# Five places in the order of work, earlier norms of the memory queries, and eight sums of squares in fp32r pairs

## The reference, cut to what matters

```python
def rms_norm(x, g):
    return x * lax.rsqrt(jnp.mean(x * x, axis=-1, keepdims=True) + NORM_EPS) * g

qa = partial_rope(rms_norm(q_a, moba_q_norm[l]), positions)      # mq: head queries
ka = partial_rope(rms_norm(k_a, moba_k_norm[l]), positions)      # mk: head keys
o_a = moba_attention(qa, ka, v_a)                                # moba
o_h = rms_norm(hgrn2_chunkwise(q_h, f_h, i_h, lb), hgrn_o_norm[l])   # ho
qm = rms_norm(q_m, mem_q_norm[l])                                # sq: memory queries
km = rms_norm(k_m, mem_k_norm[l])                                # sk: memory keys
o_m = memory_attention(qm, km, v_m)                              # matt
y = concatenate([o_a, o_h, o_m]) * silu(z)
x = x + y @ w_out[l]
```

## Time and profile before

| | |
|---|---|
| three runs, median (lowest to highest) | 1533.81 us (1533.65 to 1534.88) |
| the profiled execution | 1533.24 us |
| its span, first to last instruction | 1531.3 us |
| granted TensorE clock over the span | 1.00 |
| PE, busy share of the span | 98% |
| DVE | 76% |
| ACT | 50% |
| POOL | 7% |

### The profile page before, as it was taken

One profiled execution on the slowest core, in us unless ns is written; L12 is line 12 of the kernel. 1 busy time (PEld: TensorE's weight loads), 2 busy tenths in 40 slices (PEclk: granted clock), 3 DMA queues, 4 the chain that ended last, 5 costly groups with the idle time before them and its releaser, 6 DMA issues.

```text
span 1531.3 us, 23925 instructions
## 1 busy us (share of the span) xinstructions
PE 1495.4 (98%) x9958; PEld 1343.6 (88%) x9958; DVE 1170.6 (76%) x1392; ACT 763.8 (50%) x937; POOL 100.0 (7%) x70
## 2 busy tenths in 40 slices
PE   8999999999999999999999999999999989999988
PEld 6888899989888888888998888888999869999967
DVE  7878768757887778877677788777779676589774
ACT  5434456535433463334555544345565675555673
POOL 2000010011000010000100100001213001103000
PEclk9999999999999999999999999999999999999999
DMA  8655535214655546555433465555444314544302
GB/s 271 216 193 191 168 139 192 83 56 150 220 189 192 191 165 208 182 189 192 164 140 111 157 222 183 195 180 179 149 169 162 106 36 176 207 141 163 110 29 83
DMA packets 51888, 246.76 MB, mean 161 GB/s; under 512 B 4619, under 2 KB 5771, under 8 KB 27718
## 3 DMA queue, kind: packets, MB, share of 16 engines
q1 hardware_dynamic: 50662, 238.29, 44.7%
q0 software_dynamic: 1120, 6.96, 1.2%
HBM read 244.18 MB, written 1.05 MB: 160 GB/s over the span
## 4 chain that ended last, share of the span: by engine, by line
PE 82%; DVE 8%; ACT 5%; issue 2%; POOL 0%; DVEq 0%; ACTq 0%
PE ps L1166 20%; PE ps L1168 10%; PE ps L1089 10%; PE ps L1091 10%; PE ps L1090 10%; PE ps L1219 9%; PE ps L1220 4%; PE ps L1383 4%; PE ps L1531 1%; ACT w_hi L1638 1%; DVE w_lo L1964 1%; ACT work L1851 1%; PE ps L1520 1%; DVE act_two L2072 1%; PE ps L1499 1%
## 5 line engine op out<-in xcount | busy, mean ns | idle before, releaser
L1638 ACT ACTIVATE w_hi<-raw 128x2048 fp32r<-128x2048 f32 x184 | 351.4, 1914 | 382.7 <-PE ps L1168 267.0
L1964 DVE TENSOR_TENSOR w_lo<-raw,w_hi 128x2048 fp32r<-128x2048 f32 x177 | 405.1, 2291 | 135.2 <-ACT w_hi L1638 132.9
L1166 PE MATMUL ps<-act_two,w_hi 128*128 128x512 f32 x1408 | 444.7, 397 | 2.6 <-DVE xn L1973 1.3
L1168 PEld LDWEIGHTS ps<-act_two,w_lo 128*128 128x128 f32 x1408 | 265.3, 188 | 63.1
L1089 PE MATMUL ps<-act_two,w_hi 128*128 128x256 f32 x1088 | 318.8, 293 | 1.0 <-DVE w_lo L1958 0.9
L1091 PE MATMUL ps<-act_two,w_lo 128*128 128x256 f32 x1088 | 307.7, 283 | 0.0
L1090 PE MATMUL ps<-act_two,w_hi 128*128 128x256 f32 x1088 | 307.7, 283 | 0.0
L1168 PE MATMUL ps<-act_two,w_lo 128*128 128x256 f32 x1408 | 277.4, 278 | 0.0
L1166 PEld LDWEIGHTS ps<-act_two,w_hi 128*128 128x128 f32 x1408 | 215.3, 189 | 5.3 <-DVE xn L1973 1.7
L1089 PEld LDWEIGHTS ps<-act_two,w_hi 128*128 128x128 f32 x1088 | 208.6, 192 | 5.8 <-issue 5.1
L1090 PEld LDWEIGHTS ps<-act_two,w_hi 128*128 128x128 f32 x1088 | 208.7, 192 | 4.2 <-issue 4.1
(11 more groups left out here) (294 smaller groups left out, 2065.0 us busy)
## 6 DMA issues: line engine op xcount, KB each, us to landing
raw<-panels SPq DMA_DIRECT2D x184, 1024.0 KB, 4.8
raw<-panels SPq DMA_DIRECT2D x80, 512.0 KB, 4.9
raw<-panels SPq DMA_DIRECT2D x8, 256.0 KB, 6.5
table<-tab POOLq DMA_DIRECT2D x1, 1472.0 KB, 8.9
table<-tab POOLq DMA_DIRECT2D x1, 1216.0 KB, 5.5
xn<-x_in SPq DMA_DIRECT2D x4, 256.0 KB, 4.3
work<-mem_in POOLq DMA_DIRECT2D x1, 1024.0 KB, 9.1
xn<-mem_in POOLq DMA_DIRECT2D x1, 1024.0 KB, 5.3
```

The costliest lines, as they stand in the source:

```text
L1166: pe.matmul(grid(ps[:, bank + half], 2), w[half][0], act_two[:, slots[c]], start=c == 0, stop=False)
L1168: ins = pe.matmul(ps[:, bank + half, 0:SEQ], w[half][1], act_hi[:, slots[c]], start=False, stop=c == DC - 1)
L1638: nc.scalar.activation(w_hi[:, s], raw[:, s], ACT.Copy).then_inc(panel_hi, 1)
L1964: tt(w_lo[:, s], raw[:, s], w_hi[:, s].bitcast(F32), ALU.subtract).then_inc(panel_lo, 1)
```

## The change

1. Mixer 0: cn_sq of dq 0 is moved from behind the table load to the round of the last convolution, in front of conv_silu 4.
2. Mixer 1: norm_sum and rstd of mix1 are moved ahead of the first half of panel 1.
3. Mixer 1: scores of dilated heads 0 and 1 move one round on, behind the half panel (10, 1); the two cn_sum of fo move in front of attend of dilated heads 0 and 1.
4. Last mixer, layer 1: diagonal and diagonal_in move one round on, behind both halves of panel 7 and gap_f 0.
5. Last mixers: the norms of sq leave paired_heads and become a strand of their own from round n + 4, in front of the strand of mq, mk and ho. Their sums are written to banks 2 and 3 and wait for rope of mq 1 and of mk 1.
6. The sums of mq and mk, eight in all, are made of two fp32r products: ACT makes the Square twice, once rounded to fp32r (into g_two) and once plain, POOL subtracts to get the rest (cn_lo), and PE multiplies both with ones in fp32r (ones_r, made once beside wab_hi).
7. Every cn_sq now waits for the cn_sum two before it in the order.

```diff
+NORM_PARTS = [("pe", "cn_sum", 1), ("act", "cn_sq", 0), ("pool", "cn_lo", 0), ("act", "cn_rstd", 1), ("dve", "cn_use", 1)]
@@ hgrn_rounds
+    late = out.pop() if l else []
+    out += [[]] * l
     ahead = len(out)
...
+    out[ahead] = out[ahead] + late
@@ paired_heads
-    out[0] += pair(0, ("pe", "scores")) + [("act", "evacuate", (f"in2_{l}", 19))] + norm("cn_sq", 0, 1) + norm("cn_sum", 0, 1)
+    out[0] += pair(0, ("pe", "scores")) + [("act", "evacuate", (f"in2_{l}", 19))]
...
-        if p in (0, 1):
-            out[a] += norm("cn_rstd", p)
-        if p in (1, 2):
-            out[a] += norm("cn_use", p - 1)
@@ last_mixer
-              [[]] * n + rounds(NORM_COLS, qk + [(f"ho{l}", 0), (f"ho{l}", 1)]),
+              [[]] * (n + 4) + rounds(NORM_COLS, [(f"sq{l}", 0), (f"sq{l}", 1)]),
+              [[]] * n + rounds(NORM_PARTS, qk + [(f"ho{l}", 0), (f"ho{l}", 1)]),
...
+    chains[2] = [[x for x in r if x[1] != "cn_lo" or x[2][0] in qk] for r in chains[2]]
@@ order, mixer 0
-    conv_end = [[], [], [("dve", "conv", (5,)), ("act", "conv_silu", (4,)), ("act", "conv_silu", (5,)), ("act", "logs", ())]]
-    out += weave(conv_end + delta_rounds()[1:], halves(panel_list("in0", None, 6)), BESIDE_0)
+    conv_end = [[], [], [("dve", "conv", (5,)), ("act", "cn_sq", (("dq", 0),)), ("act", "conv_silu", (4,)), ("act", "conv_silu", (5,)), ("act", "logs", ())]]
+    rest = [[x for x in r if x != ("act", "cn_sq", (("dq", 0),))] for r in delta_rounds()[1:]]
+    out += weave(conv_end + rest, halves(panel_list("in0", None, 6)), BESIDE_0)
@@ order, mixer 1
-    out += first[:1] + [("pe", "half", ("in1", 1, 0)), ("pe", "norm_sum", ("mix1",)), ("act", "rstd", ("mix1",)), ("pe", "half", ("in1", 1, 1))]
+    out += first[:1] + [("pe", "norm_sum", ("mix1",)), ("act", "rstd", ("mix1",)), ("pe", "half", ("in1", 1, 0)), ("pe", "half", ("in1", 1, 1))]
...
-    dilated = [[]] * 4 + [two(0, ("pe", "scores")), two(0, ("dve", "mask_max"), ("act", "exp")),
+    dilated = [[]] * 5 + [two(0, ("pe", "scores")) + two(0, ("dve", "mask_max"), ("act", "exp")),
...
-                          two(0, ("pe", "attend")) + two(1, ("dve", "mask_max"), ("act", "exp")),
+                          pair(("pe", "cn_sum")) + two(0, ("pe", "attend")) + two(1, ("dve", "mask_max"), ("act", "exp")),
...
-    norms = [pair(("act", "cn_sq")), pair(("pe", "cn_sum"), ("act", "cn_rstd")), pair(("dve", "cn_use")), [("dve", "gate_out", (("dil", 0),))]]
+    norms = [pair(("act", "cn_sq")), pair(("act", "cn_rstd")), pair(("dve", "cn_use")), [("dve", "gate_out", (("dil", 0),))]]
@@ GpSimd
+            def cn_lo(unit):
+                i = norm_index[unit] % 2
+                pool.wait_ge(act_done, at("act", "cn_sq", unit))
+                hi, lo = sq_parts[i]
+                nc.gpsimd.tensor_tensor(lo, sq[i], hi.bitcast(F32), ALU.subtract).then_inc(pool_done, 1)
@@ TensorE, cn_sum
                 if unit[0][:2] == "sq":
-                    pe.wait_ge(act_done, at("act", "evacuate", "in2_" + unit[0][2], 18 + unit[1]))
+                    pe.wait_ge(dve_done, at("dve", "rope", (("mq", "mk")[unit[1]] + unit[0][2], 1)))
+                if unit in in_parts:
+                    pe.wait_ge(pool_done, at("pool", "cn_lo", unit))
+                    one, (hi, lo) = ones_r[:, int(unit[0][0] == "m")], sq_parts[norm_index[unit] % 2]
+                    pe.matmul(ps[:, bank], one, hi, start=True, stop=False)
+                    pe.matmul(ps[:, bank], one, lo, start=False, stop=True).then_inc(pe_done, 1)
+                    return
@@ ScalarE, cn_sq
+                if norm_index[unit] >= 2:
+                    act.wait_ge(pe_done, at("pe", "cn_sum", norm_list[norm_index[unit] - 2]))
...
+                if unit in in_parts:
+                    nc.scalar.activation(grid(sq_parts[norm_index[unit] % 2][0], 2), src, ACT.Square)
```

More of the change, by code:

```diff
@@ L412, in paired_heads @@
     pair = lambda p, *steps: [(e, k, ((f"moba{l}", h),)) for e, k in steps for h in (2 * p, 2 * p + 1)]
-    norm = lambda kind, *groups: [("pe" if kind == "cn_sum" else "dve" if kind == "cn_use" else "act", kind, ((f"sq{l}", g),)) for g in groups]
-    out[0] += pair(0, ("pe", "scores")) + [("act", "evacuate", (f"in2_{l}", 19))] + norm("cn_sq", 0, 1) + norm("cn_sum", 0, 1)
+    out[0] += pair(0, ("pe", "scores")) + [("act", "evacuate", (f"in2_{l}", 19))]
     for p in range(4):
@@ L539, in order @@
     heads = rounds(SCORES_FIRST, [("dif", h) for h in range(4)])
+    pair = lambda *steps: [(e, k, (("fo", g),)) for e, k in steps for g in (0, 1)]
     two = lambda p, *steps: [(e, k, (("dil", h),)) for e, k in steps for h in (2 * p, 2 * p + 1)]
-    dilated = [[]] * 4 + [two(0, ("pe", "scores")), two(0, ("dve", "mask_max"), ("act", "exp")),
+    dilated = [[]] * 5 + [two(0, ("pe", "scores")) + two(0, ("dve", "mask_max"), ("act", "exp")),
                           two(1, ("pe", "scores")) + two(0, ("dve", "divide"), ("pe", "turn_p"), ("act", "p_cols")),
-                          two(0, ("pe", "attend")) + two(1, ("dve", "mask_max"), ("act", "exp")),
+                          pair(("pe", "cn_sum")) + two(0, ("pe", "attend")) + two(1, ("dve", "mask_max"), ("act", "exp")),
                           two(1, ("dve", "divide"), ("pe", "turn_p"), ("act", "p_cols")), two(1, ("pe", "attend"))]
-    pair = lambda *steps: [(e, k, (("fo", g),)) for e, k in steps for g in (0, 1)]
-    norms = [pair(("act", "cn_sq")), pair(("pe", "cn_sum"), ("act", "cn_rstd")), pair(("dve", "cn_use")), [("dve", "gate_out", (("dil", 0),))]]
+    norms = [pair(("act", "cn_sq")), pair(("act", "cn_rstd")), pair(("dve", "cn_use")), [("dve", "gate_out", (("dil", 0),))]]
     out += weave(merge(heads, dilated, turns, [[]] * 6 + norms), halves(panel_list("in1", None, 6)), BESIDE_1)
@@ L626, in build @@
         wab_l = sb("wab_l", [P, 64], F32R)
+        ones_r = sb("ones_r", [P, 2, P], F32R)
         stat = sb("stat", [P, 120])
@@ L632, in build @@
         sq = [pair[:, 0:512], pair[:, 512:1024]]
+        sq_parts = [[g_two[:, 2 * i + j].rearrange("p a b -> p (a b)") for j in range(2)] for i in range(2)]
         rs = [pair[:, 1024:1536], pair[:, 1536:2048]]
@@ L796, in build @@
                 norms[f"mk{l}", g] = (mo_qk[:, s4], ones64, 1 / 64, sm(f"mk{l}"), mo_qk[:, s4], None, None, 1, evac(f"in2_{l}", 8 + g))
-                norms[f"sq{l}", g] = (qm[:, s2], ones, 1 / P, sm(f"sq{l}"), qm[:, s2], None, None, bank_of(f"in2_{l}", 18 + g), evac(f"in2_{l}", 16 + g))
+                norms[f"sq{l}", g] = (qm[:, s2], ones, 1 / P, sm(f"sq{l}"), qm[:, s2], None, None, 2 + g, evac(f"in2_{l}", 16 + g))
                 norms[f"sk{l}", g] = (km[:, s2], ones, 1 / P, sm(f"sk{l}"), km[:, s2], None, None, 6 + g, evac(f"mem{l}", g))
@@ L801, in build @@
                                       ("pe", "hgrn_out", l, g))
+        in_parts = [a[0] for e, k, a in ORDER if k == "cn_lo"]
         norm_list = [a[0] for e, k, a in ORDER if k == "cn_sum"]
@@ L1080, in store @@
                     pool.wait_ge(stored, 16 * TILES * 2)
-            steps("pool", {"load": load, "add": add, "zero": zero, "corner": corner, "k_level": k_level, "norm_x": norm_x, "store": store})
+            steps("pool", {"load": load, "add": add, "zero": zero, "corner": corner, "k_level": k_level, "norm_x": norm_x, "cn_lo": cn_lo, "store": store})
         @block.tensor
@@ L1673, in wab_hi @@
                 act.wait_ge(loaded["small"], 16)
+                nc.scalar.activation(ones_r[:, 0], cst("ones"), ACT.Copy)
+                nc.scalar.activation(ones_r[:, 1], cst("ones64"), ACT.Copy)
                 nc.scalar.activation(wab_h[:], sm("wab", 0, 64), ACT.Copy).then_inc(act_done, 1)
```

## The result

The changed kernel takes **1548.38 us** (median of four, 1545.10 to 1549.22) against 1533.73 for the kernel before (1532.17 to 1534.88): 1.0094 times as long, 95% interval 1.0082 to 1.0106, or 14.6 us slower. The forecast was 1541.0 with a range to 1544.5: the sign was right, the loss twice as large as told. The profiled execution has a span of 1546.2 us.

The account below looks back on a forecast made before the run. PE was taken to bound the kernel, busy 98% of the span. Parts 1 to 4 win 3.5 us and the last mixers lose 5.4 a layer, 10.8 in both: +7.3, forecast 1541.0 us, range 1535.5 to 1544.5.

Parts of the forecast that it names:

- the two waits for rope: Last mixers: PE waits 1.3 us at the sum of sq 0 and 4.1 us at that of sq 1.
- Parts 1 to 4: The four changed orders, in mixer 0, mixer 1 and layer 1's last mixer: 3.5 us won together.
- part 2: Mixer 1, norm_sum ahead of the first half panel: fills PE's wait for weights, 0.9 us won (0.6 to 0.9).
- part 4: Layer 1, diagonal one round later: two half panels cover PE's wait for k_gate, 1.0 us won (0.7 to 1.1).
- part 1: Mixer 0, cn_sq of dq 0 moved up: removes PE's 1.50 us wait, 1.0 us won (bounds 0.5 and 1.5).
- part 3: Mixer 1, dilated heads: later scores win nothing, sums of fo before the attends win 0.6 us (0 to 0.8).
- the wait for divide: Mixer 1, turn_p of differential head 3: a new wait returns the 1.37 us of the removed rope wait in full.
- the surcharge for POOL: Last mixers: 0.3 us a layer (0 to 0.9) for POOL's subtraction of mk 1 colliding with DVE's rope and copy.
- The half microsecond that the heads were to win: Heads of the last mixers: two cn_rstd fewer, 0.25 us each, 0.5 us won a layer.
- The faster one: Rival, last mixers: the last half panels hide the memory norms, so the kernel takes 1526.1 us; chance 0.13.
- Half the stall: Rival, last mixers: rope of mk 1 ends as before, 3.2 us lost a layer, 1536.7 us; chance 0.12.
- The collision at each of eight subtractions: Rival, last mixers: POOL and DVE collide at every subtraction, 0.7 us each, 5.6 in all, 1546 us; chance 0.05.

Follow-up runs that it names:

- b1_filler_three: b1_filler with 14 more products that nobody reads before the wait of scores of head 2 for mask_max of head 0; 1544.21 us, ratio 1.0069.
- b1_filler: The changed kernel with 15 and 33 products that nobody reads in front of PE's two waits for rope, in both layers; 1547.81 us, ratio 1.0094.
- a3: The kernel before with only the eight sums of mq and mk made of two fp32r products; 1532.74 us, ratio 0.9993.
- a1: The changed kernel with the norms of sq back in paired_heads, with their old banks and old wait; 1530.26 us, ratio 0.9980.
- b3: The changed kernel with the strand of sq one round later, its sums behind the last two half panels; 1534.58 us, ratio 1.0006.
- c3: b3 with 17 products that nobody reads before the wait of scores of head 2 for mask_max of head 0; 1533.67 us, ratio 0.9995.
- c1: a1 with the dilated heads of mixer 1 in their old order; 1529.64 us, ratio 0.9972.
- c4: a1 with 3, 7 and 4 products that nobody reads in PE's three waits in the dilated heads of mixer 1; 1528.42 us, ratio 0.9966.

## Why the prediction was right or wrong

**What held.** The place (the end of the last mixers), the sign, the two waits for rope and their causes. They were told as 1.3 and 4.1 us and are 1.94 in both layers (the collision below explains the difference) and 4.20 in layer 1; the 2.54 of layer 0 is the same wait, of which PE had spent a part on products at half speed. Parts 1 to 4 gave 3.3 where 3.5 was told: part 2 to the hundredth; part 4 a little over its range (1.3, told 0.7 to 1.1); part 1 0.7, as a new wait of 1 us before the transposes of the delta rule took the rest, of the kind that was priced; part 3 0.4, with the wait for divide in full, and that is partly luck, since four of eight profiles with this order have the dip and lose 1.2 there.

**The term that was missing.** No step of the sum priced the clock. The table of before says that PE's clock was at 1.00 over the span, and I carried this over to a kernel in which PE stands still three times in 20 us. b1_filler_three puts the price at 3.9 us by the layers, 4.2 by the medians and 3.8 by the ratios: two thirds of the 6.0 missed in these stages. By kind of dip: behind the waits for rope 0.2 and 1.0 (changed kernel against b1_filler), inside the heads 1.2 and 1.5 (b1_filler against b1_filler_three). The Trainium skill (TensorE: Matmul & The Clock Gate, Part 1) says that the array's clock is gated down to 1.2 GHz when the engine has not been busy and comes back when it has; the windows agree, with waits of 1.3 to 4.2 us between work as the idle time, and I had left the rule out of the prediction.

**The wait that was not followed.** I had PE reach scores of the heads with its last half panel ended at 1233.1 and called it "not last", and looked no further. Between that and mask_max at 1234.85 lies the third wait. It costs no latency of its own, since mask_max sets the time there, but it is the one behind which the longest dips come.

**The rest, 2.1 us**, is the chain of DVE. Without any dip mask_max of head 0 starts 6.7 and 6.9 us late, where 5.9 was told with the surcharge for POOL. The row is that of a3, here of the changed kernel, DVE and POOL:

```profile
1209.13 1.65 DVE L2230 TENSOR_TENSOR work<-work,xn 128x512 f32<-128x512 f32 x1
...
1208.93 1.30 POOL L1085 TENSOR_TENSOR g_two<-pair,g_two 128x512 fp32r<-128x512 f32 x1 [1.85 <-ACT pair L1856]
```

0.96 us too long, and DVE has no idle time from there to the end of rope of mq 1 at 1218.98, so it comes out at the sum of sq 0, 0.8 later than told (1218.91 in b1_filler_three, whose trace is 0.71 ahead of before there: 1218.85 - 0.71 = 1218.14). The step of the prediction that gave way is the one from cn_rstd of mk 1, told to end at 1215.9, straight to cn_use. ACT and DVE of the changed kernel there:

```profile
1214.76 0.63 ACT L1865 ACTIVATE pair<-pair 128x512 f32<-128x512 f32 x1
...
1214.92 1.23 DVE L1964 TENSOR_TENSOR w_lo<-raw,w_hi 128x1024 fp32r<-128x1024 f32 x1
1216.06 0.75 DVE L2242 SCALAR_TENSOR_TENSOR work<-work,small,pair 128x512 f32<-128x512 f32 x1
```

ACT ended at 1215.39, as told (1215.9 less the 0.59 by which this trace is ahead is 1215.3), but cn_use started at 1216.06, since DVE was still in a copy. I had priced the collision at 0.3 with a bound of 0.9, by the earlier trace rows; it came out near the bound, as DVE's operation started second and had nothing idle behind it. That this one collision is the cause is read from rows and was not tried by taking it away. The half microsecond that the heads were to win came in layer 0 (0.5) and not in layer 1 (0.2).

**The rivals.** The faster one (1526.1) took parts 1 to 4 at 3.5, the eight sums at 3.2 and the heads at 1.0. a1 is that kernel without the move, and has 3.1: of the 1.6 us a layer of the sums 0.7 is given back on DVE, and part 3 lost 1.25 with its dip instead of winning. Its condition, rope of mk 1 ended when PE comes to the sum of sq 1, failed by the wait of 4.20. Half the stall (mask_max 3.7 late) is refuted by the 6.7 without any dip. The collision at each of eight subtractions (+5.6) is refuted: in each layer one rope is held up.

**The range** failed because both its ends came from latencies. The part that decided had one unpriced term that could only lose, and no row of before could have priced it, since the last mixers held no wait of that length. The width was also less than the parts allowed: the bounds given for them (1.8 to 4.3 won, 3.2 to 6.3 lost a layer) add up to 1535.9 to 1544.6, not to 1538 to 1544.

## What to carry to other kernels

Where a change makes the engine that bounds the kernel wait, price the wait and then the work behind it at half its speed for some microseconds, and look for the following wait: it may be the costlier one though no latency hangs on it. A wait on a result that is late by one step can be made free by placing the work one round later (b3 against the changed kernel: 14 us). If a wait has to stay, products that nobody reads can be worth their place in it.

## What the runs showed of the hardware

That the clock falls on waits so short. The changed kernel's PE waited 1.3 to 4.2 us at a time and its clock fell to 0.50 for 3 to 7 us. In a1 it fell for 3 us behind waits of 0.39, 0.92 and 0.61 that lie within 3 us of one another, in c3 behind 0.26 and 0.91. It is not fixed: with equal waits four profiles of eight had the dip in mixer 1, and the wait of 1.94 had one behind it in layer 0 of the changed kernel and none in layer 1. Nor does it need a changed order: in c1 it fell for 3 us in the heads of layer 1 behind waits of 0.26, 0.56 and 0.46, and with the same waits in a1 and c4 it did not. What tells these apart stays open. A dip of 3 us in mixer 1 costs 1.6 us (1.24 lost against 0.36 won).

Parts add up well when read by the shifts of a common instruction: the move and the sums alone, 8.6 - 0.95 and 10.1 - 0.93, give the 7.6 and 9.2 of the whole.
